# Third layer's first norm: ScalarE squares each residual tile as it arrives, instead of waiting for all eight

## The chip, the cores and the metric

The kernel runs on one core of one Trainium2 chip. The metric is the device time of one execution in microseconds (us). Lower is better.

## What is computed

Three transformer-like blocks follow each other on one sequence of 512 positions and 1024 channels. The change sits where the second block ends and the third begins. Cut to what matters:

```python
# end of the second block
f = jnp.square(jax.nn.relu(h @ w_ff1[l])) @ w_ff2[l]
x = x + rmsnorm(f, norm_ffn_post[l])
...
# start of the third block
def rms_norm(x, g): ...          # x * rsqrt(mean(x * x, channels) + eps) * g
mod = (c_act @ w_ada[l] + b_ada[l])[:, None, :]
sh1, sc1, gt1, sh2, sc2, gt2 = jnp.split(mod, N_MOD, axis=-1)
h = rms_norm(x, g_norm1[l]) * (1.0 + sc1) + sh1
u = h @ w_in[l]
q, k, v, iq, ik, iw, ca, cg = jnp.split(u, split_pts, axis=-1)
```

So the third block's first norm needs, for every position, the sum over all 1024 channels of the squares of the x that the second block's last addition makes.

## The kernel before

Activations lie with channels on the 128 partitions: `X` is the residual stream in eight tiles of 128x512 (channel tile k, all 512 positions), and `H` is a second tensor of the same size. Weights arrive as slabs of 128x1024 in a ring of four. Each fp32 slab is split by ScalarE into a rounded high part (`w_high`, line 326) and by GpSimd into the rest (`w_low`, line 357), and TensorE multiplies three products of high and low parts for each 128x128 block (line 388). Each engine runs its own program, written out stage by stage; semaphores with counts tie them together. Nothing is reordered by a scheduler: what stands in the Python functions is the order on the engine.

**Around the change**, in this order:

- The second block's last stage ends with `post_norm_dve`. For each of the eight tiles VectorE scales f (line 2257) and adds it to X (line 2259). Each such addition raises the semaphore `x_ready` by one. `x_ready` counts all updates of X since the start: eight for each of seven updates by then, so that it goes from 48 to 56 in this one.
- `three_act` (ScalarE) starts the third block with `act.wait_ge(x_ready, 7 * DT)`, DT being 8, and then calls `pre_norm_act`. That one squares each X tile into H (line 554), loads the activation table (line 490), and takes the inverse root as a logarithm (line 492) and an exponential (line 493) into `root`.
- `norm_pe` (TensorE) waits for each square and multiplies it by a matrix of ones into PSUM bank `aux` 0, one fp32 product for each tile, which the profile shows as two MATMUL instructions (line 565). The last raises `sum_ready`, for which line 492 waits.
- `modulated_norm_dve` (VectorE) waits for `root` and makes H from X, the gain and `root` (line 2818). `high_act` (ScalarE) adds the shift (line 405) and rounds (line 407), and VectorE takes the low part (line 416).
- `three_pe` then runs the stage `in3a` from the rounded parts. Its first weight tile has, for each k, eight small fp32 products for `iw` (line 2557) ahead of the three products of line 388.
- `three_pool` (GpSimd) splits two slabs, waits for `x_ready` to be 56, issues two DMAs of rotation tables (lines 2505 and 2506), and goes on splitting slabs.

The functions that carry the norm on ScalarE are these. They are the same for the norm ahead of the second block's feed-forward part, which follows the same `post_norm_dve`, and which has no wait ahead of `pre_norm_act`:

```python
def x_wait(eng, count):
    base = count.x - DT
    def wait(k):
        if base >= 0:
            eng.wait_ge(x_ready, base + k + 1)
...
def norm_act(act, a, n, src, sq, src_wait, scale, eps="eps", root_wait=None, first=None):
    for k in range(n):
...
        src_wait(k)
        nc.scalar.activation(sq(k), src(k), ACT.Square).then_inc(sq_ready, 1)
...
    inverse_root(act, a, scale, eps)
```

Of the kernel before, what the change touches and what calls it, by code (L numbers as in the profile page):

```python
# [28 lines left out]
DT = D // P  # L29
# [181 lines left out]
def build(nc, d, out):  # L211
    ctx = ExitStack()
    with ctx:
        sems = {}

        def sem(name):
            if name not in sems:
                sems[name] = ctx.enter_context(nc.semaphore(name))
            return sems[name]
# [58 lines left out]
        x_ready = sem("x_ready")  # L278
# [322 lines left out]
        n_pe, n_act, n_dve = Count(), Count(), Count()  # L601
# [16 lines left out]
        def pre_norm_act(act, a, first=None):  # L618
            norm_act(act, a, DT, Xk, Hk, x_wait(act, n_act), 1.0 / D, first=first)
            n_act.x += DT  # L620
# [2086 lines left out]
                products(t, range(DT)).then_inc(slab_done, 1)  # L2707

        def three_act(act, a):
            act.wait_ge(x_ready, 7 * DT)  # L2710
            pre_norm_act(act, a)
            high_act(act, a, tiles_of(H3_high), 0, True)
            act.wait_ge(iw_psum, 1)
# [268 lines left out]
        def load_slabs(sp, lo, hi, beside=None):  # L2982
# [29 lines left out]
            (final1_pe, final1_act, final1_dve, None, ()),  # L3012
            (two_pe, two_act, two_dve, two_pool, ()),
            (three_pe, three_act, three_dve, three_pool, ()),
        ]
        X_UPDATES = 1 + 1 + 1 + 1 + 1 + 2 + 3
# [316 lines left out]
```

## Time and profile before

| | us |
|---|---|
| median of 3 runs | 3378.77 |
| fastest and slowest of them | 3377.24, 3387.88 |
| the profiled execution, its own time | 3377.85 |
| its span, first to last instruction | 3376.0 |
| TensorE busy in it | 3202.6 (95%) |

The span is cut into stretches by the engines' waits. The profile gives the busy time of each engine, the chain of work that ended last, followed back through what released each step, a timeline of instructions, and the granted TensorE clock as a share of full speed (0.50 is 1.2 GHz, 1.00 is 2.4 GHz). An instruction's row gives its start, its length, its line, what it writes and reads, and in brackets how long its engine was idle before it and what released it.

### The profile page before, as it was taken

The numbers are of one execution on the slowest core, as the hardware profiler recorded it, in microseconds if no ns is written. First come the engines' busy times: TensorE is split into PE (matmuls) and PEld (weight loads), VectorE is DVE, ScalarE is ACT, GpSimd is POOL, SyncE is SP. The second block draws the span as 40 slices with busy tenths as digits, with TensorE's granted clock in tenths as the row PEclk, the third lists the DMA queues.
The fourth block names the chain that finished last, engine by engine and source line by source line (L and its number), as shares of the span: only waits on it lengthen the run. The fifth ranks groups of instructions, "written<-read, shape, count | busy, mean of one in ns | idle before, by whom it ended". The sixth has DMA issues, their size and how long they took to land.

```text
span 3376.0 us, 62851 instructions
## 1 busy us (share of the span) xinstructions
PE 3202.6 (95%) x25640; PEld 2430.3 (72%) x25640; DVE 1578.3 (47%) x2342; ACT 1133.1 (34%) x1623; POOL 1203.3 (36%) x612
## 2 busy tenths in 40 slices
PE   7999999979899999999988999989998999999999
PEld 5757888848688887777766856458886774448887
DVE  6755553194255545677130421444152576636060
ACT  5413443212433333443233313232222334632221
POOL 3323444424144412444433422024443264314443
PEclk9999999989899999999999999999999899999999
DMA  3212333313000001555332322113332121023333
GB/s 135 81 38 82 99 94 100 106 55 95 12 3 3 3 24 60 193 183 179 123 98 73 95 68 62 50 61 95 100 94 81 50 71 36 1 62 94 100 93 100
DMA packets 73073, 266.37 MB, mean 79 GB/s; under 512 B 8207, under 2 KB 8218, under 8 KB 72704
## 3 DMA queue, kind: packets, MB, share of 16 engines
q1 hardware_dynamic: 72000, 260.32, 24.3%
q0 software_dynamic: 896, 3.52, 0.3%
q8 instruction: 132, 2.16, 0.3%
q14 instruction: 45, 0.37, 0.0%
HBM read 261.71 MB, written 2.10 MB: 78 GB/s over the span
## 4 chain that ended last, share of the span: by engine, by line
PE 75%; issue 10%; DVE 7%; POOL 4%; ACT 3%; DMA 0%; POOLq 0%; DVEq 0%; SPq 0%; ACTq 0%
PE gp L388 53%; POOL w_low L357 4%; PE gp L1227 4%; PE gp L2174 2%; PE gp L314 2%; PE gp L2678 2%; PE aux L1353 1%; PE aux L1227 1%; PE gp L1985 1%; PE gp L2637 1%; PE gp L2655 1%; PE aux L1994 1%; PE aux L565 1%; DVE arena L1667 1%; DVE aux L2858 1%
## 5 line engine op out<-in xcount | busy, mean ns | idle before, releaser
L357 POOL TENSOR_TENSOR w_low<-ring,w_high 128x1024 fp32r<-128x1024 f32 x397 | 955.9, 2408 | 1755.8 <-ACT w_high L326 1755.8
L326 ACT ACTIVATE w_high<-ring 128x1024 fp32r<-128x1024 f32 x397 | 420.1, 1059 | 1345.1 <-PE gp L388 1287.6
L388 PE MATMUL gp<-ffn_h,w_high 128*128 128x512 f32 x2432 | 757.4, 393 | 12.7 <-DVE ffn_h L418 5.1
L388 PEld LDWEIGHTS gp<-ffn_h,w_high 128*128 128x128 f32 x2432 | 455.1, 189 | 123.7 <-POOL w_low L357 12.5
L388 PE MATMUL gp<-ffn_h,w_low 128*128 128x512 f32 x1216 | 474.9, 391 | 0.0
L388 PE MATMUL gp<-ffn_high,w_high 128*128 128x512 f32 x928 | 361.9, 390 | 3.3 <-POOL w_low L357 3.2
L388 PE MATMUL gp<-ffn_high,w_low 128*128 128x512 f32 x864 | 336.9, 390 | 0.0
L388 PE MATMUL gp<-ffn_low,w_high 128*128 128x512 f32 x864 | 336.7, 390 | 0.0
L388 PEld LDWEIGHTS gp<-ffn_h,w_low 128*128 128x128 f32 x1216 | 229.1, 188 | 48.0
L2102 DVE TENSOR_TENSOR arena<-arena 128x512 f32<-128x512 f32 x64 | 152.9, 2389 | 200.3 <-ACTq L163 200.3
L388 PE MATMUL gp<-in_h,w_high 128*128 128x512 f32 x768 | 239.6, 393 | 4.7 <-DVE in_h L416 4.7
L388 PEld LDWEIGHTS gp<-ffn_high,w_high 128*128 128x128 f32 x928 | 174.6, 188 | 41.0 <-POOL w_low L357 4.0
L388 PEld LDWEIGHTS gp<-ffn_high,w_low 128*128 128x128 f32 x864 | 162.5, 188 | 33.7
L388 PEld LDWEIGHTS gp<-ffn_low,w_high 128*128 128x128 f32 x864 | 162.6, 188 | 33.5
L388 PEld LDWEIGHTS gp<-in_h,w_high 128*128 128x128 f32 x768 | 144.8, 189 | 38.3 <-issue 6.2
L388 PE MATMUL gp<-in_h,w_low 128*128 128x512 f32 x384 | 150.3, 392 | 0.0
L388 PE MATMUL gp<-hyena_high,w_high 128*128 128x512 f32 x320 | 129.6, 405 | 16.3 <-POOL w_low L357 14.0
L388 PE MATMUL gp<-hyena_high,w_low 128*128 128x512 f32 x320 | 126.4, 395 | 0.0
L1083 ACT ACTIVATE arena<-gp,par 128x512 f32<-128x512 f32 x88 | 68.0, 773 | 119.9 <-DVEq L163 119.9
L2825 DVE SCALAR_TENSOR_TENSOR X<-gp,par,X 128x512 f32<-128x512 f32 x24 | 18.0, 751 | 184.4 <-PE gp L388 152.6
L388 PE MATMUL gp<-h_low,w_high 128*128 128x512 f32 x256 | 101.5, 397 | 0.0
L646 DVE TENSOR_TENSOR X<-gp,X 128x512 f32<-128x512 f32 x16 | 11.1, 692 | 192.4 <-PE gp L388 192.4
(470 smaller groups left out, 5166.6 us busy)
## 6 DMA issues: line engine op xcount, KB each, us to landing
ring<-in_weights SPq DMA_DIRECT2D x437, 512.0 KB, 3.6
H<-in_ada SPq DMA_DIRECT2D x48, 512.0 KB, 4.3
X<-in_x SPq DMA_DIRECT2D x4, 512.0 KB, 7.5
out_x<-X SPq DMA_DIRECT2D x8, 256.0 KB, 4.8
arena<-in_sm POOLq DMA_DIRECT2D x1, 1024.0 KB, 5.0
cst<-in_cst SPq DMA_DIRECT2D x1, 756.0 KB, 9.9
arena<-in_hy_f_w POOLq DMA_DIRECT2D x1, 512.0 KB, 4.5
arena<-in_hy_delta POOLq DMA_DIRECT2D x1, 512.0 KB, 6.4
```

Of the source, the lines that this page charges most:

```text
L314: last = nc.tensor.matmul(gp[0:width, t.bank, :], ring[:, slab % RING, i * P:i * P + width], rhs(k, t), start=(k == 0), stop=(k == sum(kt) ...
L326: nc.scalar.activation(w_high[:, slab % PARTS, :], ring[:, slab % RING, :], ACT.Copy).then_inc(high_ready, 1)
L357: nc.gpsimd.tensor_tensor(w_low[:, slab % PARTS, :], ring[:, slab % RING, :], w_high[:, slab % PARTS, :], ALU.subtract).then_inc(low_ready, 1)
L388: last = nc.tensor.matmul(gp[:, t.bank, :], wt[:, slab % PARTS, w], x(k), start=(k == 0 and q == 0), stop=(k == sum(kt) - 1 and q == 2))
L565: last = nc.tensor.matmul(aux[:, 0, :], ones, sq(k), start=(k == 0), stop=(k == n - 1))
L1083: nc.scalar.activation(tmp, z, ACT.Identity, scale=ff_cols(layer, t, 1), bias=pcol("ff_conv_b", layer * 2 * F1T + t.idx)).then_inc(aff_rea ...
L1227: return nc.tensor.matmul(out[HEADS[cols]], lhsT[HEADS[rows]], rhs[HEADS[rows]], start=start, stop=True, skip_group_check=True)
L1353: last = nc.tensor.matmul(out, XS[d][HEADS[p], half4(h, j)], const("eye64")[HEADS[p], :], start=True, stop=True, skip_group_check=True)
L1667: return nc.vector.scalar_tensor_tensor(out=arena[:, (wMA, wMB)[m % 2] + i if m < 3 else (wLA, wLB)[m % 2] + i, :], in0=arena[:, wXX + i, ...
L2102: v(nc.vector.tensor_tensor(f, f, f, ALU.mult))
L2174: last = nc.tensor.matmul(gp[:, t.bank, :], ring[:, slab % RING, t.j * P:(t.j + 1) * P], arena[:, bOUT + 2 * b + k, :], start=(k == 0), st ...
L2678: last = nc.tensor.matmul(gp[:, t.bank, :], ring[:, (st.slab0 + t.j) % RING, i * P:(i + 1) * P], arena[:, dAT + i, :], start=(i == 0), sto ...
```

## The change

ScalarE's wait for all eight tiles is taken out of `three_act`. In its place stands a check made while the program is built, which issues nothing: the count of X updates that `pre_norm_act` starts from is 56, so that its own wait for tile k is for `x_ready` of 48 + k + 1.

```diff
         def three_act(act, a):
-            act.wait_ge(x_ready, 7 * DT)
+            assert n_act.x == 7 * DT
             pre_norm_act(act, a)
             high_act(act, a, tiles_of(H3_high), 0, True)
             act.wait_ge(iw_psum, 1)
```

No instruction is added or moved on any engine: each engine's instructions stand in the order in which they stood.

## Rows read from the trace of the kernel before

**Rows 1.** The page's part 1, the whole execution

```profile
PE 3202.6 (95%) x25640; PEld 2430.3 (72%) x25640; DVE 1578.3 (47%) x2342; ACT 1133.1 (34%) x1623; POOL 1203.3 (36%) x612
```

**Rows 2.** The chain that ended last, 2590 to 2640 us: start, length, what

```profile
2606.41 0.70 DVE X L2259
...
2607.14 0.64 ACT H L554
...
2607.91 8.72 PE aux L565 x16
...
2616.65 0.69 ACT root L492
...
2618.12 0.76 DVE H L2818
...
2621.16 1.65 PE aux L2557 x8
2622.81 1.48 PE gp L388 x3
```

**Rows 3.** Who waited for whom, 2590 to 2660 us: total, times, longest

```profile
ACT H L554 <- DVE X L2259: 11.3, 1, 11.3
```

**Rows 4.** ScalarE's timeline ahead of the third block

```profile
2611.42 1.28 ACT L490 ACT_TABLE_LOAD   x1
2616.65 0.69 ACT L492 ACTIVATE root<-aux,cst 128x512 f32<-128x512 f32 x1 [3.95 <-PE aux L565]
```

**Rows 5.** VectorE's timeline, first additions to X of this update

```profile
2596.70 0.69 DVE L2259 TENSOR_TENSOR X<-X,arena 128x512 f32<-128x512 f32 x1
...
2598.08 0.69 DVE L2259 TENSOR_TENSOR X<-X,arena 128x512 f32<-128x512 f32 x1
```

**Rows 6.** ScalarE's timeline, the norm after the second block's first update

```profile
2224.40 0.63 ACT L554 ACTIVATE H<-X 128x512 f32<-128x512 f32 x1 [1.54 <-DVE X L2259]
...
2234.12 0.63 ACT L554 ACTIVATE H<-X 128x512 f32<-128x512 f32 x1 [0.76 <-DVE X L2259]
2234.77 1.28 ACT L490 ACT_TABLE_LOAD   x1
2236.07 0.69 ACT L492 ACTIVATE root<-aux,cst 128x512 f32<-128x512 f32 x1
```

**Rows 7.** VectorE's timeline in the same place

```profile
2223.68 0.69 DVE L2259 TENSOR_TENSOR X<-X,arena 128x512 f32<-128x512 f32 x1
...
2233.40 0.69 DVE L2259 TENSOR_TENSOR X<-X,arena 128x512 f32<-128x512 f32 x1
```

**Rows 8.** TensorE's timeline in the same place

```profile
2225.18 6.59 PE L565 MATMUL aux<-H,cst 128*128 128x512 f32 x10 [3.80 <-ACT H L554]
...
2234.81 1.12 PE L565 MATMUL aux<-H,cst 128*128 128x512 f32 x2 [0.26 <-ACT H L554]
```

**Rows 9.** Busy time by stretch (PE, PEld, DVE, ACT, POOL), PEclk, DMA share, GB/s

```profile
2225.20:2228.90 3.70, 3.70 (x5) 1.49 (x6) 3.63 (x6) 1.59 (x3) 0.00 (x0) 0.54 0.00 0
...
2597.50:2611.10 13.60, 3.19 (x4) 1.51 (x5) 9.61 (x16) 3.96 (x8) 1.12 (x2) 0.50 0.12 39
2611.10:2621.30 10.20, 5.65 (x15) 2.27 (x13) 3.06 (x5) 5.24 (x8) 0.00 (x0) 1.00 0.00 0
2621.40:2643.60 22.20, 22.20 (x86) 20.18 (x85) 7.40 (x13) 7.62 (x13) 0.00 (x0) 0.50 0.00 1
2643.60:2648.70 5.10, 5.10 (x13) 4.04 (x14) 0.00 (x0) 2.19 (x5) 2.28 (x1) 0.50 0.31 103
```

**Rows 10.** TensorE's weight loads in the norm of the third block

```profile
2609.75 0.34 PEld L565 LDWEIGHTS aux<-H,cst 128*128 128x128 f32 x1 [0.52 <-issue]
2610.60 0.34 PEld L565 LDWEIGHTS aux<-H,cst 128*128 128x128 f32 x1 [0.52 <-ACT H L554]
2611.30 0.19 PEld L565 LDWEIGHTS aux<-H,cst 128*128 128x128 f32 x1 [0.36 <-issue]
2611.73 0.19 PEld L565 LDWEIGHTS aux<-H,cst 128*128 128x128 f32 x1 [0.24 <-issue]
```

## The prediction

> **What bounds the kernel now.** I read the page's part 1 first. TensorE is busy for 3202.6 us of the span of 3376.0 us [rows 1], so time can be won only in the 173 us in which it stands still, or where it runs at half clock. Then I read the chain of work that ended last, around the seam between the second and the third block. The reader is to see there that the norm's steps stand one behind the other: the last addition to X ends at 2607.11, the squares begin at 2607.14, TensorE's sixteen MATMULs for the sums of squares take 8.72 us, and only then comes the logarithm, at 2616.65 [rows 2]. All of this is on the chain. From the end of the last addition to the logarithm it is 2616.65 - 2607.11 = 9.54 us.
>
> The view of waits says what ScalarE did before: it sat idle 11.3 us until VectorE had finished X [rows 3]. But the tiles came one by one. The first addition ended at 2596.70 + 0.69 = 2597.39, the second 1.38 us later [rows 5]. So seven of the eight squares, and seven of the eight products with the ones, could have been done beside the additions.
>
> **What the change does.** It takes that one wait out. No instruction is added, removed or moved, and no DMA. What is left to hold ScalarE is its wait for each tile. The price need not be guessed, since the same helpers run once more in this trace, without the extra wait, at 2224 us. There the additions are as far apart (2223.68 to 2233.40 is 9.72 us for seven steps, 1.39 us each [rows 7]), the first square starts at 2224.40, 0.03 us behind its tile, with 0.63 us for each [rows 6]. TensorE starts at 2225.18 and does its last pair from 2234.81 for 1.12 us [rows 8]. The last addition ends at 2233.40 + 0.69 = 2234.09 and the logarithm starts at 2236.07 [rows 6, 7]: 1.98 us.
>
> The sum, step by step:
> - Additions on VectorE: unchanged, 0 us. That ScalarE now squares beside them doesn't slow them: 1.39 us apart with the squares beside them [rows 7], 1.38 us without [rows 5].
> - From the last addition to the logarithm: 9.54 - 1.98 = 7.56 us less. The logarithm should start at about 2609.1.
> - The table load of 1.28 us [rows 4] lies today under TensorE's products (from 2611.42, while the logarithm waits 3.95 us for TensorE). That cover goes. In the earlier norm the load ends at 2236.05 and the last pair of products at 2235.93, so the load is what is late next. It stands already in the 1.98 us.
> - From the logarithm on nothing is changed: root, H, shift, rounding, low part, and TensorE's first product of the in-projection 4.51 us after the logarithm starts (2621.16 - 2616.65 [rows 2]). That product should come at about 2613.6.
> - The first weight tile of the in-projection: TensorE is busy throughout, from 2621.4 to 2643.6, at PEclk 0.50 [rows 9]. It sets its own pace: for each of eight k the small products and then the large ones, which take 1.48 us [rows 2], follow with no gap. It starts earlier and is as long: 0 us.
> - Weight slabs: the first two are split before the norm ends, and DMA share is 0.00 over that tile [rows 9], so nothing late in the stream can take the place of the wait. GpSimd still waits for the eighth tile before its two rotation DMAs, as before: 0 us. Later splits and loads wait for TensorE's progress and move with it.
>
> The sum is 7.56 us less. Against the profiled execution's 3377.85 us that gives 3370.3; that execution lies 0.92 us below the median shown. From the median it is 3378.77 - 7.56 = 3371.2 us, which is 0.22% less. About 0.3%, or 10.1 us, is what a measurement of this kernel can tell from no change, so I call this "the same" though I expect a true gain.
>
> **Two rules of the Trainium skill against the rows.** The first is about the table. In the trace the earlier norm goes from the last square (ends 2234.75) to the load at 2234.77 and from its end at 2236.05 to the logarithm at 2236.07 [rows 6]: the load costs its 1.28 us and no more, and the sum uses that. The Trainium skill, ScalarE: Activation LUTs, section What ACT_TABLE_LOAD costs, adds a drain of about 1.38 us to each load; by it the load, now uncovered, would leave some 6.2 us of the gain (an estimate from that page). With that rule the trace does not agree; it is also the fourth rival.
>
> The second is about the clock. The norm's dense block of products did two things in the kernel before: it began at half clock and went to full at about 2611.1, and full clock then held to 2621.3 [rows 9]. The in-projection, starting at 2621.16, got nothing of it: it ran at 0.50 for 22.2 us. So the sum takes no loss from thinning that block. The Trainium skill, TensorE: Matmul & The Clock Gate, section What's actually happening, says that the throttled state is the default and that activity releases it; by this rule, products spread thin beside the additions might not release it at all. By this rule the sum would be that of the second rival below. The rows of the earlier norm speak against it: half clock to about 2228.9 (PEclk 0.54 up to there [rows 9]), and the last pair at 1.12 us, against the 1.70 us that a pair needs at half clock.
>
> **The rivals.**
> 1. *Full clock reaches the in-projection.* If the clock does not fall in TensorE's pause before the in-projection (last product near 2609.0, first at 2613.6, 4.6 us), the first tile runs at up to double pace. At full clock it would save half of 22.2 us, 11.1 us, so 18.7 us in all: 3360.1 us. If only a part of the tile or of the 5.1 us of half clock behind it [rows 9] goes, the saving is between, say 11 us: 3367.8. For it: the tile is wholly bound by TensorE. Against it: the pause before was 4.53 us (2607.91 + 8.72 = 2616.63 to 2621.16 [rows 2]) and the clock was down right behind its end; the pause now is about as long. The tile didn't bring it up in 22 us either. Chance of a gain beyond 10.1 us in all: 0.19.
> 2. *Half clock through the whole norm.* At half clock weight loads of the products are 0.85 us apart, 1.70 us for a pair; at full clock 0.43, 0.86 us for a pair [rows 10]. At 1.70 TensorE is slower than the tiles come. The first square would be ready at about 2598.1, and eight pairs end at 2598.1 + 8 x 1.70 = 2611.7: the logarithm starts at 2611.8 instead of 2609.1, and the gain is 4.9 us: 3373.9 us. At full clock all the way TensorE is never behind and the 7.56 stands; these are the two ends for this cost, and the earlier norm [rows 8] is nearest to the upper one. Chance 0.08.
> 3. *The wait removed was no wait.* Something else would have to hold the first square, or the logarithm, until 2616.65. Nothing does: root was free, and 11.3 us of ScalarE's idle time is put down to X [rows 3]. Then 3378.8. Chance 0.02.
> 4. *The table load costs more once nothing covers it.* Before, from its start to the logarithm there were 2616.65 - 2611.42 = 5.23 us [rows 4], in which a longer load would not have shown. If it took all of them, the logarithm would start at 2607.8 + 5.23 = 2613.0, the gain would be 3.6 us and the time 3375.2. Against it: 1.28 us from load to end, then 0.02 us to the logarithm, where nothing covered it either [rows 6]. Chance 0.02.
> 5. *Slower: the clock comes back later in dense work.* After the first tile the in-projection is dense, and half clock lasts another 5.1 us [rows 9]. Every us of dense work at half clock costs 0.5 us. Shifting the program by 7.6 us shifts where each pause falls, here and in the attention and at the last norm. It would take 15.1 us more of half clock to eat the gain, and 35.3 us more to be slower by 10.1 us: 3388.9 us. For it: the runs shown spread by 10.6 us with no edit, and one of them stands at 3387.88. Against it: behind the first tile, dense work stood at half clock for 5.1 us only [rows 9]. The DMAs and the slabs of this stretch give no other such mechanism. Chance 0.03.
>
> **How the numbers follow.** My forecast is the 7.56 us, with a spread of some 2 to 3 us for the clock (the 5.1 us of half clock may shrink or grow by half, 1.3 us, here and in each of a few later places): chance 0.66, nearly all of it inside 0.3%. With the second, third and fourth rival that makes 0.78 for "the same"; the first gives 0.19 for faster; the fifth 0.03 for slower. The predicted time is that of the forecast, 3371.2 us. The range takes in the second and the fourth rival, up to 3378.0, and part of the first, down to 3365.0. Left out are most of the full-clock case and the slower one.
>
> **What would show each step.** In the profile after: squares of line 554 in eight rows 1.39 us apart, each idle 0.76 us until VectorE's addition, the first at about 2597.4; TensorE's line 565 from about 2598.1; line 492 some 2.0 us behind the last addition rather than 9.54; line 2557 first at about 2613.6, if the start of the seam stays where it was. GpSimd's two DMAs stay right behind the eighth addition. The prediction is wrong if line 492 still waits several us for TensorE (rival 2), if PEclk is above 0.50 over the first tile (rival 1), or if the stages behind show more half clock than before (rival 5).

## The result

The change made the kernel faster, by more than was forecast.

| | before | changed |
|---|---|---|
| median of 20 runs, us | 3387.41 | 3375.09 |
| fastest and slowest | 3377.24, 3394.04 | 3370.18, 3378.29 |
| profiled execution, its own time | 3377.85 | 3370.18 |
| its span | 3376.0 | 3368.4 |

The ratio of the runs is 0.9964, with a 95% interval of 0.9956 to 0.9972. Against the median of 3387.41 that is 12.2 us less, between 9.5 and 14.9. The two profiled executions are 7.67 us apart. So one pair of profiles shows the gain that was forecast, 7.56 us, and twenty runs show some 4.6 us more. Note also what the first three runs hid: their median was 3378.77, and that of twenty is 8.6 us higher. The profile that the prediction rests on is among the fastest executions of its kernel. One run of the later kernel `before_plus2` took 4076.52 us at a granted clock of 0.740, and it is left out of that kernel's figures.

**The profile of the changed kernel** at the seam. First the chain that ended last (start, length, what), which answers to [rows 2]:

```profile
2606.46 0.70 DVE X L2259
...
2607.18 0.63 ACT H L554
...
2607.83 1.28 ACT L490
...
2609.13 0.70 ACT root L492
...
2610.59 0.76 DVE H L2818
...
2613.64 1.82 PE aux L2557 x8
```

TensorE's sums (line 565, 8.72 us before) are gone from the chain. The table load has taken their place, with 1.28 us. From the end of the last addition to the logarithm it is 1.98 us by the timeline (2607.15 to 2609.13), after 9.55 in the kernel before (the prediction read 9.54 off the chain). The rest of the way to TensorE's first product of the in-projection is what it was, 4.51 us.

ScalarE's timeline of the same stretch, and TensorE's:

```profile
2597.47 0.63 ACT L554 ACTIVATE H<-X 128x512 f32<-128x512 f32 x1 [1.54 <-DVE X L2259]
2598.86 0.63 ACT L554 ACTIVATE H<-X 128x512 f32<-128x512 f32 x1 [0.76 <-DVE X L2259]
...
2607.18 0.63 ACT L554 ACTIVATE H<-X 128x512 f32<-128x512 f32 x1 [0.76 <-DVE X L2259]
2607.83 1.28 ACT L490 ACT_TABLE_LOAD   x1
2609.13 0.69 ACT L492 ACTIVATE root<-aux,cst 128x512 f32<-128x512 f32 x1
```

```profile
2598.24 7.97 PE L565 MATMUL aux<-H,cst 128*128 128x512 f32 x12 [3.80 <-ACT H L554]
2606.48 1.13 PE L565 MATMUL aux<-H,cst 128*128 128x512 f32 x2 [0.26 <-ACT H L554]
2607.87 1.12 PE L565 MATMUL aux<-H,cst 128*128 128x512 f32 x2 [0.26 <-ACT H L554]
```

Each square starts 0.03 us behind its tile, and ScalarE's longest wait for X has fallen from 11.3 us to 1.5. TensorE lags at first and has caught up by the seventh tile. The reader may lay these rows beside [rows 6, 8]: the earlier norm foretold ScalarE's to the hundredth. TensorE caught up one tile later than there (twelve MATMULs before the first wait, against ten), at no cost to the logarithm. GpSimd's rotation DMAs stay 0.30 us behind the last addition, as before.

The windows of the changed kernel (busy PE, PEld, DVE, ACT, POOL, then PEclk, DMA share, GB/s):

```profile
2596.60:2603.40 6.80, 5.16 (x6) 2.14 (x7) 6.63 (x11) 2.90 (x5) 0.00 (x0) 0.50 0.00 0
...
2613.70:2636.40 22.70, 22.70 (x86) 20.67 (x87) 7.58 (x13) 7.79 (x13) 0.00 (x0) 0.50 0.00 1
2636.40:2641.00 4.60, 4.60 (x11) 3.59 (x12) 0.00 (x0) 2.19 (x5) 1.93 (x1) 0.50 0.36 112
...
2688.80:2692.10 3.30, 3.30 (x8) 2.15 (x8) 1.33 (x3) 0.79 (x3) 0.00 (x0) 0.50 0.00 0
```

The clock was at half when the first sum began and came back to full 5.2 us later, at 2603.4. That cost nothing, since the work lay beside the additions. The first tile of the in-projection is at 0.50 throughout, as before [rows 9].

### The profile page after: what moved, and what is told of

It reads as the page before. It is cut to its first block, busy times and chain, and to the rows that moved or that the text cites. A ratio compares the mean times of both kernels' runs of the same rounds, so it can differ in the third digit from the quotient of the medians.

```text
span 3368.4 us, 62850 instructions
## 1 busy us (share of the span) xinstructions
PE 3206.5 (95%) x25640; PEld 2434.2 (72%) x25640; DVE 1575.6 (47%) x2342; ACT 1134.2 (34%) x1623; POOL 1203.6 (36%) x612
## 4 chain that ended last, share of the span: by engine, by line
PE 75%; issue 10%; DVE 7%; POOL 4%; ACT 3%; DMA 0%; POOLq 0%; DVEq 0%; ACTq 0%; SPq 0%
PE gp L388 53%; POOL w_low L357 4%; PE gp L1227 4%; PE gp L2174 2%; PE gp L314 2%; PE gp L2678 2%; PE aux L1353 1%; PE aux L1227 1%; PE gp L1985 1%; PE gp L2637 1%; PE gp L2655 1%; PE aux L1994 1%; DVE arena L1667 1%; DVE aux L2858 1%; PE aux L1222 1%
## 5 line engine op out<-in xcount | busy, mean ns | idle before, releaser
L646 DVE TENSOR_TENSOR X<-gp,X 128x512 f32<-128x512 f32 x16 | 11.1, 692 | 191.9 <-PE gp L388 191.9
```

## The experiments

Twelve experiments follow. The ratio given for each is to the kernel before, run on the same chip (its median stood at 3387.11, 3389.48 and 3388.35 us on the three chips used).

### Is it TensorE's block, and what varies from run to run?

Four kernels: the two as they are, once more, and two that undo a part of the change.

`pe_holds`, in the changed kernel:

```diff
         def three_pe(pe):
+            pe.wait_ge(sq_ready, n_pe.sq + DT)
             norm_pe(pe, DT, Hk)
```

> The changed kernel, but TensorE waits for all eight squares before its first product of ones; ScalarE squares each tile as it arrives. Theory: the gain comes from TensorE's products running beside the additions. Then this kernel has its dense block back behind the last addition, logarithm about 9.5 us behind it, and the time of the kernel before. Rival (the gain lies in ScalarE's squares): 0.63 us is all that ScalarE can be on the path, and the kernel would be near the changed one, 12 us below the kernel before.

Measured: 3385.42 beside 3387.11, ratio 0.9990 (0.9979 to 1.0000). Its TensorE row, and ScalarE's last square and logarithm:

```profile
2610.86 9.81 PE L565 MATMUL aux<-H,cst 128*128 128x512 f32 x16 [13.43 <-ACT H L554]
```

```profile
2610.18 0.63 ACT L554 ACTIVATE H<-X 128x512 f32<-128x512 f32 x1 [0.76 <-DVE X L2259]
...
2620.71 0.69 ACT L492 ACTIVATE root<-aux,cst 128x512 f32<-128x512 f32 x1 [8.60 <-PE aux L565]
```

Each square follows its own tile, the block is back, and the logarithm is 10.56 us behind the last addition. What is left of the gain is 3.4 us by the ratio, with 0 to 7.1 us in its interval, against 12.2. So most of the gain, and all of it that the trace shows on this path, lies in TensorE's products beside the additions.

`wait_four`, in the kernel before:

```diff
-            act.wait_ge(x_ready, 7 * DT)
+            act.wait_ge(x_ready, 7 * DT - 4)
             pre_norm_act(act, a)
```

> The kernel before with its wait set to four tiles instead of eight. The fourth addition ends at about 2601.6; squares of four tiles follow at 0.53 us each and TensorE starts at about 2602.4. Half clock lasts some 3.3 us (two pairs at 1.70), then pairs at 0.86: six more end at about 2611. The logarithm at about 2611, 4 us behind the last addition: 5.5 us of the 7.56 are gained. If the gain is all or nothing (a state that the long pause of TensorE sets), it would be either 0 or the whole.

Measured: 3381.51 beside 3387.11, ratio 0.9984 (0.9974 to 0.9994), so 5.4 us. The additions of this execution end at 2615.78:

```profile
2611.04 9.36 PE L565 MATMUL aux<-H,cst 128*128 128x512 f32 x16 [7.96 <-ACT H L554]
```

```profile
2620.43 0.69 ACT L492 ACTIVATE root<-aux,cst 128x512 f32<-128x512 f32 x1 [2.69 <-PE aux L565]
```

The logarithm is 4.65 us behind them (4 were forecast), between 1.98 and 9.55. The gain comes in part and is not all or nothing.

`before_again`, the kernel before:

> The kernel before, unchanged, to see what varies from run to run. If the change gains only the 7.6 us of the serial norm, its spread has nothing to do with the norm, and the logarithm starts 9.5 us behind the last addition in every profile. If the time that TensorE's dense block of sums needs varies with the moment at which the clock comes back, that 9.5 us varies: 8.72 us for the block at 3.2 us of half clock, 8.72 + 0.5 x the further us of half clock, so 10 to 11 us at most, and the median of this kernel lies 1 to 2 us above its fastest run for that reason.

`after_again`, the changed kernel:

> The changed kernel, unchanged. Logarithm 2.0 us behind the last addition again, in any profile. Serial theory alone: 7.6 us below the fast profiles of the kernel before, and about the same spread. If the clock's return mattered only in the dense block: 8 to 9 us below the median of before, with a narrower spread. If something else is at work behind the seam: 12 us below, and the profiles differ after the in-projection starts.

Measured: 3388.99 (3380.33 to 3393.62) for the kernel before, and 3374.78 (3373.18 to 3375.98), ratio 0.9958 (0.9945 to 0.9971), for the changed one. The kernel before has its median 8.7 us above its fastest run, where 1 to 2 were forecast; between the two kernels it is the third forecast, something else behind the seam, that came. This pair of profiles is what the first pair was not: 3389.81 against 3374.78, 15 us apart. Cut at the same instructions, from the timelines of the four executions, in us:

| piece | before | before_again | changed | after_again |
|---|---|---|---|---|
| start to the last addition's end | 2607.1 | 2614.0 | 2607.2 | 2616.0 |
| from there to the first product of line 2557 | 14.06 | 15.13 | 6.49 | 6.48 |
| from there to the last of them (first tile) | 22.19 | 22.39 | 22.36 | 22.39 |
| from there to the last product of the in-projection | 147.64 | 154.18 | 147.45 | 147.28 |
| from there to the end | 585.05 | 582.29 | 584.90 | 580.84 |

Read the two columns of the kernel before. The first row differs by 6.9 us and the last by 2.8, the other way. The first lies ahead of the change, where the instructions are the same, and the changed kernel's two executions differ in it by 8.8 us. So it is spread of the runs and not worth of the change, but it is the largest part of what one profile hides. It was not followed further, and nor was the last row, which runs from 580.8 to 585.1 us over the four.

Of the rows between, two differ. The second: the block of sums started at half clock in each, but took 8.72 us in the first profile and 9.78 in this one, because full clock came later:

```profile
2614.83 9.78 PE L565 MATMUL aux<-H,cst 128*128 128x512 f32 x16 [13.52 <-ACT H L554]
```

The fourth row differs more, by 6.5 us, and the place of it lies some 80 us behind the change. There TensorE stands still 3.7 us for VectorE's rotation, and then does index products of 64x256 between blocks of large ones. TensorE's timeline of before_again, and of the changed kernel:

```profile
2703.94 1.13 PE L2585 MATMUL aux<-arena 64*128 64x256 f32 x6 [3.74 <-DVEq L163]
...
2707.41 1.22 PE L2585 MATMUL aux<-arena 64*128 64x256 f32 x2
...
2710.14 1.22 PE L2585 MATMUL aux<-arena 64*128 64x256 f32 x2
```

```profile
2687.81 1.18 PE L2585 MATMUL aux<-arena 64*128 64x256 f32 x6 [3.73 <-DVEq L163]
...
2693.47 0.70 PE L2585 MATMUL aux<-arena 64*128 64x256 f32 x2
...
2694.99 0.70 PE L2585 MATMUL aux<-arena 64*128 64x256 f32 x2
```

One pair to the next is 2.73 us in the one and 1.52 in the other. The window of before_again (PEclk, third figure from the end, is 0.50) says why:

```profile
2705.60:2722.60 17.00, 17.00 (x34) 9.26 (x33) 6.32 (x14) 3.84 (x8) 2.42 (x2) 0.50 0.09 31
```

After the pause the clock falls in every one of the four. In three it is back after some 3.4 us (the short course), and in before_again it stayed at half for 17 us (the long course). The pause is equally long in all. What differs is the moment: the clock fell 0.95 us behind the first index product in the changed kernel (2687.81 to 2688.76) and 1.60 us behind it in before_again (2703.94 to 2705.54). `pe_holds` (1.64 us behind) and `wait_four` (0.00) also had the long course, 17.1 and 20.5 us of it. Over all nine profiles here that have this pause: the six in which the clock fell 0.28 to 1.16 us behind the product took the short course, and the three at 0.00, 1.60 and 1.64 the long one. That is what goes together in nine traces; the moment was not set at will in any of them, so that it is the cause is not shown.

So a second thing may part the two kernels: which of the two courses the clock takes further on. That was a new theory, called below the theory of place, and the next experiments test it against the serial theory, by which only the path from the last addition to the logarithm counts.

### A delay that should make it faster

In each, a number of copies on ScalarE that serve nothing, ahead of the logarithm of this norm (`n_act.delay` is set to that number around this one norm, and is 0 for all others):

```diff
             act.wait_ge(sum_ready, n_act.sums)
+            for _ in range(n_act.delay):
+                a(nc.scalar.activation(dst, X[:, DT - 1, :], ACT.Copy))
```

`before_plus2`, two copies in the kernel before:

> The kernel before, with two copies of a 128x512 tile on ScalarE between TensorE's sums and the logarithm: work that serves nothing, 1.3 us on the path. Theory of place: the profiles so far differ behind the seam in where the clock falls around TensorE's first index product (3.4 us of half clock where it falls 0.9 to 1.2 us behind that product's start, 17.1 us where it falls 1.6 us behind), and 1.3 us more moves the seam to where the short one follows: the median is lower than that of the kernel before in spite of the added work, 1 to 5 us lower. Rival (the rest of the gain is in TensorE's block of sums, or is chance): 1.3 us slower, 3388.4.

Measured: 3384.44 beside 3389.48, ratio 0.9988 (0.9979 to 0.9998), which is 4.1 us less, between 0.7 and 7.1. The kernel with 1.3 us of useless work on its path is faster, by a margin whose lower end is small. ScalarE's rows and the window behind the first index product (which starts at 2702.15):

```profile
2622.72 1.29 ACT L493 ACTIVATE root<-X 128x512 f32<-128x512 f32 x2 [3.85 <-PE aux L567]
2624.04 0.69 ACT L494 ACTIVATE root<-aux,cst 128x512 f32<-128x512 f32 x1
```

```profile
2702.40:2705.80 3.40, 3.40 (x11) 2.22 (x10) 1.32 (x3) 1.04 (x3) 0.00 (x0) 0.50 0.00 0
2705.90:2722.00 16.10, 16.10 (x68) 11.02 (x66) 9.47 (x25) 5.57 (x10) 5.06 (x4) 1.00 0.22 66
```

The copies are on the path, full clock is back after 3.4 us, the clock fell 0.28 us behind the first index product, and the fourth piece of the table is 146.93 us. A theory of a merely serial norm asks for 1.3 us more, a ratio of 1.0004, and that lies outside the interval. That the short course is what made the eleven runs faster rests on one profile; the delay moves everything behind it, and the runs don't say in which piece the time was won.

`after_plus1` and `after_plus3`, one and three copies in the changed kernel:

> The changed kernel with one such copy, 0.65 us on the path. Serial theory: 0.65 us slower than the changed kernel, 3375.6. Theory of place: the same, or up to 6.6 us more if the seam falls already where the long half clock follows.

> The changed kernel with three such copies, 2.0 us on the path. Serial theory: 3377.0, same spread. Theory of place: the seam comes to lie, against the clock's moments, as in the slow profiles of the kernel before, so 17.1 us of half clock behind the first index product and 6.6 us more: 3383 to 3385, with a granted clock of 0.970 instead of 0.974.

Measured: 3377.14 (3372.28 to 3380.89), ratio 0.9965 (0.9948 to 0.9981), and 3380.53 (3372.69 to 3384.87), ratio 0.9976 (0.9963 to 0.9988). One copy gave 2.05 us for 0.65, which both forecasts allow. With three copies the median is 3.5 us above what the copies cost, and single runs reach 3384.9 at a granted clock of 0.970 to 0.972. But the forecast of 3383 to 3385 for its median was missed, and its one profile (3372.69) shows 3.4 us of half clock at that place. So the theory offers a mechanism and does not foretell, for a given shift, how many runs take the long course. The table shows one reason: from run to run the seam itself comes as much as 8.9 us earlier or later, so a delay of 0.65 to 2 us can't put the clock's fall at a chosen moment.

### Without the pause

`index_later`, the changed kernel with its first eight index heads later:

```diff
-        IN3B_INDEX = {(1, 3): (0, 1, 2), (1, 5): (3,), (1, 6): (4,), (1, 7): (5,), (2, 0): (6,), (2, 1): (7,),
+        IN3B_INDEX = {(2, 1): (0, 1, 2), (2, 3): (3,), (2, 4): (4,), (2, 5): (5,), (2, 6): (6,), (2, 7): (7,),
```

> The changed kernel with the first eight index heads put six blocks of products later in the in-projection (from tile 1 to tile 2 of its second stage), so that TensorE does not stand still 3.7 us for VectorE's rotation in front of them. Theory of place: without that pause the clock does not fall there at all: 3.7 us of pause and 1.7 us of half clock go, 5 us less than the changed kernel, 3370, if the heads' results are not needed earlier by VectorE. Rival: VectorE waits for the heads and all behind it comes later; then the same or some us slower.

Measured: 3369.33 (3367.69 to 3371.95), ratio 0.9942 (0.9929 to 0.9956). From where half clock ends, 5 us behind the first tile, to the end of the in-projection:

```profile
2647.20:2795.00 147.80, 147.80 (x639) 107.86 (x639) 112.69 (x196) 47.63 (x71) 78.91 (x45) 1.00 0.24 72
```

TensorE has no pause in it and full clock throughout. VectorE's wait for the heads' results did not grow into a new bound: the fourth piece is 142.2 us, 5 less than the short course had.

With the pause gone the two courses are gone, and the original question can be asked with less in the way. `before_index` is the kernel before with that same edit, `index_again` the one above once more, both on the same chip:

> The kernel before, wait for eight tiles and all, with the first eight index heads later in the in-projection, so that TensorE has no pause there. Theory: 12 us between the two kernels are 7.6 us of the serial norm, about 1 us of half clock in its block of sums, and the rest from the long half clock behind the first index product, into which most runs of the kernel before fall and the changed kernel's don't. With the pause gone in both, before and changed lie 8 to 9 us apart: this one at 3377 to 3379 beside 3369 to 3370. Rival (the long half clock is not what parts them): they stay 12 us apart, and this one is at 3381 or more.

> The changed kernel with the later heads, once more, beside the others on the same chip: 3369 to 3370, granted clock 0.974 to 0.975, and no half clock between the first tile of the in-projection and the attention.

Measured: 3377.66, ratio 0.9972 (0.9961 to 0.9982), and 3367.97, ratio 0.9949 (0.9935 to 0.9964). They are 9.7 us apart by the medians and 7.8 by the ratios (0.9949 / 0.9972 = 0.9977). The forecast was 8 to 9 and the rival's 12; `index_again` itself came 1 us under its forecast. The first ratio is known to some 3.6 us and the second to some 4.9, so this leans to the forecast and does not exclude 12. The same edit is worth 10.7 us to the kernel before (3388.35 to 3377.66) and about 6 to the changed one (3375.09 to 3369.33, on different chips): more in the kernel in which the long course was seen, as the theory asks.

### The clock by itself

`before_warm_index`: in `before_index`, TensorE's pause ahead of the sums is filled.

```diff
         def three_pe(pe):
+            for _ in range(14):
+                nc.tensor.matmul(aux[:, 3, :], ones, cst[:, 0:S], start=True, stop=True)
             norm_pe(pe, DT, Hk)
```

> The kernel before with the later heads, and fourteen fp32 products that serve nothing on TensorE in its pause ahead of the norm's sums, 0.86 us each at full clock, 12 us in all, so that the clock should be full when the block of sums begins. Theory: the block takes 6.9 us instead of 8.7 to 9.8, the logarithm starts 7.8 us behind the last addition instead of 9.5 to 10.6, and this kernel is 2 to 3 us faster than the one with the later heads alone: 3375. Rival (the half clock in the block costs nothing that counts): the same as that one.

Measured: 3374.82, ratio 0.9966 (0.9954 to 0.9978). By the medians that is 2.8 us under `before_index` on the same chip, by the ratios 2.0; their intervals overlap, so the times alone don't exclude the rival. The trace speaks for the theory:

```profile
2601.31 12.18 PE L2552 MATMUL aux<-cst 128*128 128x512 f32 x28
2614.99 7.10 PE L565 MATMUL aux<-H,cst 128*128 128x512 f32 x16 [1.50 <-ACT H L554]
```

The block takes 7.10 us, all at full clock, and the logarithm comes 7.95 us behind the last addition instead of 10.72. So half clock in this block cost 1.6 us on this path in the first profile of the kernel before (9.55 to 7.95), and 2.8 in `before_index`.

`index_warm`: in `index_later`, five such products between the last sum and the first tile.

```diff
             norm_pe(pe, DT, Hk)
+            for _ in range(5):
+                nc.tensor.matmul(aux[:, 3, :], ones, cst[:, 0:S], start=True, stop=True)
```

> The changed kernel with the later heads, and five such products on TensorE between the norm's last sum and the in-projection's first tile, 4.3 us at full clock in a pause of 4.65 us. Asks whether full clock can live in the first tile. If it can: the tile's 22.4 us become 12 to 15 and the time 3360 to 3363. If the tile itself lets the clock fall (it did not bring it up in 22 us): the gain is a few us of full clock at its start, 1 to 2 us, 3368.

Measured: 3361.35 (3352.26 to 3366.07), ratio 0.9929 (0.9912 to 0.9946): the fastest kernel of this study, 27.0 us under the kernel before and 6.6 under `index_again` by the medians on its chip. Its first tile, and that of index_again:

```profile
2616.50:2629.00 12.50, 12.48 (x87) 11.55 (x88) 7.68 (x13) 8.21 (x16) 0.00 (x0) 1.00 0.01 1
```

```profile
2617.70:2641.00 23.30, 23.06 (x86) 21.07 (x87) 7.89 (x14) 8.36 (x15) 0.00 (x0) 0.50 0.00 1
```

From the start of the first to the start of the last of the small products for `iw` (line 2557 of the kernel before) it is 11.88 us at full clock, and 22.39 at half. The tile does not bring the clock up, nor did it let it fall here. That profile is the fastest run. Of its six runs three are at 3352 to 3357 with a granted clock of 0.979 to 0.981, and three at 3366 with 0.974; that the latter lost full clock in this tile is likely, but none of them was profiled.

## Why the prediction was right, and where it fell short

- **The serial norm, 7.56 us: right in size and mechanism.** In the profiles the way from the last addition to the logarithm went from 9.55 to 1.98 us, 7.57 less, and the executions are 7.67 us apart. In before_again and after_again it went from 10.62 to 1.97. Taking the price from the earlier norm of the same kernel was what made it exact, the uncovered table load with it.
- **Which part holds it: right.** `pe_holds` shows that ScalarE's own early squares are worth little without TensorE's products (3.4 us, 0 to 7.1, of 12.2).
- **Additions, slabs, first tile at 0 us: right.** Additions stay 1.39 us apart, the first tile took 22.36 us after 22.19, and TensorE went from the logarithm to it in 4.51 us as before, so no slab was waited for.
- **The step that failed is the term for the clock:** "a spread of some 2 to 3 us", taken as equal on both sides, from one execution. It had two parts that are not. The block of sums took 8.72 us in the profile read, but 9.8 in before_again, `pe_holds` and `before_index`, and the change hides that too: 1 us more. This part is shown. And some 80 us on, one of the two profiles of the kernel before, and both kernels that undo a part of the change, had a long stretch at half clock, 6.5 us dearer, which neither profile of the changed kernel showed. The rest of 12.2, some 3.6 us, is what that makes if it happens in about half of the runs; that share is worked out from the medians and not counted. That removing the pause brings the two kernels to 7.8 to 9.7 us apart supports it and does not prove it, and why the changed kernel should take the short course more often stays open.
- **The baseline.** I took the 3378.77 of three runs as the middle. It is 8.6 us under that of twenty. The predicted 3371.2 came within 3.9 us of 3375.09 and the range held it by luck, since two errors were opposite: the baseline was taken too low and the gain too small. From 3387.41 the same 7.56 us would have given 3379.9, above the range's end of 3378.0. On whether the gain is within 0.3%, on which I put 0.78, the runs don't decide: they give 0.36%, with 0.28% to 0.44% as its interval.
- **The rivals.** The first, full clock in the first tile, did not come with this change (PEclk 0.50), but its price did: 11.1 us reckoned, 10.5 measured in `index_warm`. The second, half clock in the norm, came for the first 5.2 us of the sums and then ended in time. (The text against it sets 1.12 us, a pair's length, beside 1.70, the distance from pair to pair at half clock; the like of 1.70 is 0.86 us. The reading is the same.) The third, that the wait was none, is refuted by ScalarE's early squares and the logarithm 1.98 us behind the addition. The fourth, a dearer uncovered load, is refuted: 1.28 us and 0.02 to the logarithm. The fifth had the mechanism that the runs point to, a shift that changes where pauses meet the clock, and the wrong sign: it helped. Its ground against itself, that dense work had stood at half clock for 5.1 us only, was one profile's: 17.1 us stood in the next.

## What to carry to other kernels

- Where a helper is used twice, once with an extra wait and once without, read the price of the wait from the other use; here it came out to 0.01 us.
- When runs of one kernel spread by 17 us, a profile shows one run of many. Take a second one, cut both at the same instructions, and see which piece differs, before the gain of a shift by a few us is believed or explained.
- Look at what TensorE does just before a stretch that it alone sets: products that serve nothing, in a pause that exists anyway, were worth 10.5 us here in the one profile in which they kept full clock, and 6.6 us by the medians of the runs.

## What was not expected of the hardware

- A program became some 4 us faster (ratio 0.9988, 0.9979 to 0.9998) when 1.3 us of useless work was put on its path. Its one profile has the short course of the clock 80 us further on; that this is why is inferred.
- Work in which small products alternate with large ones kept the clock where it was: with a pause of 4.5 to 6.6 us ahead of it, the tile of it took 21.6 to 22.4 us, nearly all at half clock, in thirteen profiles, and 11.9 us at full clock in the one profile where that pause was filled.
- After a pause of 3.7 us of one and the same length, half clock lasted 3.4 us in six profiles, 17.1 us in two and 20.5 us in one, according to where the clock fell against the first product behind the pause.
